# Ends of the layers, low parts in two halves, one chunk taken earlier and query sums in column groups, in a block of two mixer layers and a feed-forward block

## The chip, the cores and the metric

One core of a Trainium2 chip runs the whole program. The metric is the device time in microseconds (us). Five engines matter here: TensorE (PE in the profile, with PEld for its weight loads), VectorE (DVE), ScalarE (ACT), GpSimd (POOL), and SyncE (SP), which only issues the transfers of weights.

## What is computed

The input has 512 rows of 1024 features, all in float32. First come two layers of this form:

```
h    = rms_norm(x) * (1 + scale) + shift
proj = h @ w_in                         # gq gk gv | low rank | gz | dq dk dv dz
o_gla  = rms_norm(gated linear attention(silu(conv(gq, gk, gv)))) * silu(gz)
q, k   = rms_norm(dq) per half head of 64, rms_norm(dk)
attn   = softmax(q1 k1) - lam * softmax(q2 k2)      # 4 heads, causal by chunks
o_diff = rms_norm(attn @ dv) * silu(dz)
x      = x + gate * (concat(o_gla, o_diff) @ w_out)
```

Then follow a gated feed-forward (1024 to 2816 to 1024), a mixer with a spatial gating branch and a short convolution branch, a second feed-forward and a last rms_norm.

## The kernel before

**Products.** Every float32 product of a weight is made as three products of rounded parts (`products`, lines 890 to 897): high weight by high data (L895), high by low (L896), low by high (L897). Where the data are the stationary side the same three stand at L927 to L929. Weights come in chunks of 128 x 2048 (128 x 1408 for the second product of a feed-forward) through two buffers `raw[0]`, `raw[1]`. SP loads a chunk (L463) once the chunk two before it was split. ACT makes its high part `wh` (`take_high`, L543), then POOL its low part `wl` as `raw` minus `wh` in one instruction (`split`, L499), which tells PE and SP through the semaphore `w_ready`.

**Units.** One chunk is one unit of work for PE: two tiles of 128 x 512 in two PSUM banks. `claim` waits until both banks of a unit are emptied, `chunk_ready` until the whole low part is there.

**Layers.** The order inside a layer is a list, `ORDER`, made by `layer_order` (L80). It holds the 56 quarter units ("parts") of the projections, and after part n the small stages that were `put` at n. PE, ACT and DVE all walk the same list in program order; each does its share of a stage. Around the change the list has:

- 29 to 34: sums of squares of the queries. DVE squares them (`q_squares`, L1720), PE sums halves of heads with 16 products of 2 columns from `sq` and 16 from `tmp` (`q_sums`, L1243), ACT takes the root (`q_norm`, L740).
- 35 to 53: 16 attention steps `attn`, each with `score` (L1107), `biases` on DVE (L1627 to L1629, the last of which multiplies two 128 x 2 operands in SBUF into `nbias`), `exps` on ACT, `combine` on DVE (L1639), `turn` (L1116) and `pv` (L1129) on PE.
- 51 to 55: `z_act` (Silu of z on ACT, L768), `gated_r` and `gated_z` (DVE, L1611 and L1619), `diff_ss` (sums for the norm of the attention output, L1604 and L1605), `diff_root` (its root on ACT, L771), and `mix` 0 to 3 (PE transposes at L1082, ACT makes high parts at L658, DVE low parts at L1647).

Behind the list PE waits for the low parts of the first four mixes, claims the banks of both units, and begins the output product with its gla half (`first_out`), with the transposes 4 to 7 of the attention half (`turn_output`) between its pieces. The last quarter of z is emptied by ACT at part 55 (`empty`, L650) straight into Silu; that emptying is what frees the second pair of banks. Behind it ACT takes the next chunk.

**Norms.** `norm(n)` between stages: PE sums squares (L1016, L1020), ACT takes the root (L600) and then the high part of the stage's second chunk, DVE makes a diagonal from two operands in SBUF (L1429), PE spreads it (L1027). For n = 2, 3 and 4 (feed-forward 1, mixer, feed-forward 2; `splits=False`) PE starts the first unit before the norm is known and has the spread behind it.

Of the kernel before, what the change touches and what calls it, by code (L numbers as in the profile page):

```python
# [25 lines left out]
F32 = mybir.dt.float32  # L26
# [5 lines left out]
P = 128  # L32
# [8 lines left out]
HEADS = 4  # L41
# [36 lines left out]
def layer_order():  # L78
# [31 lines left out]
    put(33, "q_squares", (2, 3))  # L110
    put(33, "turn_keys", (0, 1))
    put(34, "q_sums")
    put(34, "turn_keys", (2, 3))
    put(34, "q_norm")
    for s in range(STEPS + 3):
        put(35 + s, "attn", s)
        if s >= 6 and s % 4 == 2:
            put(36 + s, "diff_ss", 3 - (s - 6) // 4)
    for tb in range(TB):
        put(36 + tb, "gated_r", 0, tb)  # L120
    put(51, "z_act", 0)
# [47 lines left out]
def build(nc, ins, out):  # L169
    ctx = ExitStack()  # L170
    with ctx:  # L171
# [32 lines left out]
        inhalf = sb("inhalf", [P, 2])  # L204
        eps = sb("eps", [P, 3])
        sumsq = sb("sumsq", [P, S])
# [116 lines left out]
        w_ready = sem("w_ready")  # L323
        half_used = sem("half_used")
# [44 lines left out]
        q_ss = sem("q_ss")  # L369
        q_scaled = sem("q_scaled")  # L370
# [80 lines left out]
        def _(sp):  # L451
# [31 lines left out]
        def _(pool):  # L483
# [28 lines left out]
        def _(act):  # L512
# [83 lines left out]
            def norm(n, splits=True):  # L596


                act.wait_ge(norm_ss, n + 1)
                nc.scalar.activation(norm_sd[:], ps[:, 6, 0:TB], ACT.Sqrt, bias=eps[:, 0:1],  # L600
                                     scale=1.0 / D).then_inc(norm_root, 1)
                first = (0, CHUNK0["layer1"], CHUNK0["ffn1"], CHUNK0["mixer"], CHUNK0["ffn2"], CHUNKS)[n]
# [13 lines left out]
                take_high(first + 1)  # L616
                if splits:
                    for k in range(KT):
# [10 lines left out]
            for l in range(LAYERS):  # L629
# [58 lines left out]
                for stage, *at_ in ORDER:  # L688
# [45 lines left out]
                    elif stage == "k_norm":  # L734
                        act.wait_ge(k_var, l + 1)
                        nc.scalar.activation(r_qk[:, 0], ss_k[:], ACT.Sqrt, bias=eps[:, 0:1], scale=1.0 / DK
                                             ).then_inc(k_root, 1)
                    elif stage == "q_norm":
                        act.wait_ge(q_ss, l + 1)
                        nc.scalar.activation(r_qk[:, 1].rearrange("p b g -> p (b g)"), ps[:, 5, 0:32], ACT.Sqrt,  # L740
                                             bias=eps[:, 0:1], scale=1.0 / DK).then_inc(q_root, 1)
# [149 lines left out]
        def _(pe):  # L891
# [10 lines left out]

            def chunk_ready(i, chunk, u):
                pe.wait_ge(w_ready, i * 2 + (chunk + u + 1))
# [1076 lines left out]
```

## Time and profile before

| | |
|---|---|
| median of 3 runs | 1829.73 us (1824.44 to 1832.11) |
| the profiled execution, its own time | 1827.28 us |
| its span, first to last instruction | 1825.5 us |
| PE busy | 1760.1 us (96%) |
| DVE, ACT, POOL busy | 939.9, 646.0, 661.9 us |
| mean granted TensorE clock | 0.99 |

Busy PE is not PE at its peak. What is read here is therefore where PE stands idle and what ended each wait, and then, in a timeline of the engines around such a place, what the releaser itself had waited for. In a timeline row the first number is the start, the second the duration, the bracket the idle time ahead and its releaser.

### The profile page before, as it was taken

The numbers are of one execution on the slowest core, as the hardware profiler recorded it, in microseconds if no ns is written. First come the engines' busy times: TensorE is split into PE (matmuls) and PEld (weight loads), VectorE is DVE, ScalarE is ACT, GpSimd is POOL, SyncE is SP. The second block draws the span as 40 slices with busy tenths as digits, with TensorE's granted clock in tenths as the row PEclk, the third lists the DMA queues.
The fourth block names the chain that finished last, engine by engine and source line by source line (L and its number), as shares of the span: only waits on it lengthen the run. The fifth ranks groups of instructions, "written<-read, shape, count | busy, mean of one in ns | idle before, by whom it ended". The sixth has DMA issues, their size and how long they took to land.

```text
span 1825.5 us, 22633 instructions
## 1 busy us (share of the span) xinstructions
PE 1760.1 (96%) x9017; PEld 1447.4 (79%) x9017; DVE 939.9 (51%) x895; ACT 646.0 (35%) x801; POOL 661.9 (36%) x163
## 2 busy tenths in 40 slices
PE   5999999899999999999999999999999999999997
PEld 2677797688888788888888988888888788888885
DVE  4657657777665555554232346672223555554233
ACT  4332563344455433333333332232222433333221
POOL 2232233333222444443444444434444344443442
PEclk9999999899999999999999999999999999999998
DMA  8563112122111222322222332222222222232221
GB/s 335 208 237 108 47 64 74 51 86 74 47 70 47 88 96 92 103 103 70 96 95 87 115 115 92 92 92 92 92 92 92 83 102 92 97 110 71 95 95 62
DMA packets 29660, 180.79 MB, mean 99 GB/s; under 512 B 4342, under 2 KB 4476, under 8 KB 12060
## 3 DMA queue, kind: packets, MB, share of 16 engines
q1 hardware_dynamic: 24480, 161.50, 25.2%
q10 hardware_dynamic: 5116, 18.39, 2.8%
q8 instruction: 46, 0.75, 0.2%
q14 instruction: 18, 0.15, 0.0%
HBM read 177.78 MB, written 2.10 MB: 99 GB/s over the span
## 4 chain that ended last, share of the span: by engine, by line
issue 65%; PE 19%; POOL 15%; POOLq 0%; DVE 0%; ACT 0%; DVEq 0%; ACTq 0%
POOL wl L499 15%; PE ps L897 6%; PE ps L896 6%; PE ps L895 6%; DVE y L1441 0%; POOLq L504 0%; PE ps L1027 0%; POOLq L498 0%; ACT L600 0%; PE ps L1020 0%; DVE sq L1429 0%; DVEq L171 0%; ACT sq L572 0%; POOL glr L487 0%; ACTq L171 0%
## 5 line engine op out<-in xcount | busy, mean ns | idle before, releaser
L499 POOL TENSOR_TENSOR wl<-raw,wh 128x2048 fp32r<-128x2048 f32 (+1 forms) x152 | 659.9, 4342 | 1136.5 <-ACT wh L543 1136.5
L895 PE MATMUL ps<-xh,wh 128*128 128x512 f32 x1280 | 503.8, 394 | 12.9 <-DVE xl L1404 5.6
L896 PE MATMUL ps<-xl,wh 128*128 128x512 f32 x1280 | 499.4, 390 | 0.0
L897 PE MATMUL ps<-xh,wl 128*128 128x512 f32 x1280 | 499.4, 390 | 0.0
L543 ACT ACTIVATE wh<-raw 128x2048 fp32r<-128x2048 f32 x152 | 291.1, 1915 | 495.3 <-PE ps L897 457.7
L895 PEld LDWEIGHTS ps<-xh,wh 128*128 128x128 f32 x1280 | 240.9, 188 | 75.9 <-issue 24.3
L897 PEld LDWEIGHTS ps<-xh,wl 128*128 128x128 f32 x1280 | 240.8, 188 | 51.0
L896 PEld LDWEIGHTS ps<-xl,wh 128*128 128x128 f32 x1280 | 241.1, 188 | 48.9
L1802 DVE TENSOR_TENSOR fl<-tmp,fh 128x512 f32 x44 | 194.9, 4431 | 84.7 <-ACT fh L799 84.7
L927 PE MATMUL ps<-wh,xh 128*128 128x256 f32 x576 | 169.0, 293 | 1.5 <-POOL wl L499 1.5
L928 PE MATMUL ps<-wh,xl 128*128 128x256 f32 x576 | 163.6, 284 | 0.0
L929 PE MATMUL ps<-wl,xh 128*128 128x256 f32 x576 | 163.5, 284 | 0.0
L897 PE MATMUL ps<-fh,wl 128*128 128x512 f32 x352 | 140.4, 399 | 0.0
L896 PE MATMUL ps<-fl,wh 128*128 128x512 f32 x352 | 138.7, 394 | 0.0
L895 PE MATMUL ps<-fh,wh 128*128 128x512 f32 x352 | 138.0, 392 | 0.0
L927 PEld LDWEIGHTS ps<-wh,xh 128*128 128x128 f32 x576 | 110.9, 193 | 20.1 <-issue 19.1
L928 PEld LDWEIGHTS ps<-wh,xl 128*128 128x128 f32 x576 | 111.0, 193 | 0.0
L929 PEld LDWEIGHTS ps<-wl,xh 128*128 128x128 f32 x576 | 110.9, 193 | 0.0
L1418 DVE TENSOR_TENSOR sumsq<-sumsq,sq 128x512 f32<-128x512 f32 x36 | 84.1, 2337 | 41.1 <-ACT sq L572 40.4
L1797 DVE TENSOR_TENSOR tmp<-ps,gate 128x512 f32<-128x512 f32 x44 | 30.5, 692 | 134.0 <-PE ps L897 131.8
L791 ACT ACTIVATE gate<-gate 128x512 f32<-128x512 f32 x44 | 27.9, 633 | 195.8 <-DVE gate L1792 195.8
L1485 DVE TENSOR_TENSOR gate<-ps,r_bc 128x512 f32<-128x512 f32 x16 | 11.1, 691 | 149.6 <-PE ps L897 149.6
(241 smaller groups left out, 2160.5 us busy)
## 6 DMA issues: line engine op xcount, KB each, us to landing
raw<-ffn_in_stream SPq DMA_DIRECT2D x44, 1024.0 KB, 4.8
raw<-mixer_stream SPq DMA_DIRECT2D x40, 1024.0 KB, 4.8
raw<-layer_stream SPq DMA_DIRECT2D x36, 1024.0 KB, 4.9
raw<-ffn_out_stream SPq DMA_DIRECT2D x32, 704.0 KB, 4.1
ada_w<-w_ada SPq DMA_DIRECT2D x8, 1024.0 KB, 18.6
ada_late<-w_ada ACTq DMA_DIRECT2D x16, 512.0 KB, 5.2
ada_late<-w_ada ACTq DMA_DIRECT2D x8, 1024.0 KB, 6.9
x<-x_t SPq DMA_DIRECT2D x1, 2048.0 KB, 7.5
```

The lines of the kernel that those rows point to most:

```text
L499: nc.gpsimd.tensor_tensor(wl[u][:, 0:size], raw[u][:, 0:size], wh[u][:, 0:size].bitcast(F32), ALU.subtract).then_inc(w_ready, 1)
L543: nc.scalar.activation(wh[u][:], raw[u][:], ACT.Copy).then_inc(w_high, 1)
L791: nc.scalar.activation(gate[:, u], gate[:, u], ACT.Silu).then_inc(ff_gate, 1)
L895: nc.tensor.matmul(bank_ap, w0, x0, start=first, stop=False)
L896: nc.tensor.matmul(bank_ap, w0, x1, start=False, stop=False)
L897: return nc.tensor.matmul(bank_ap, w1, x0, start=False, stop=last)
L927: nc.tensor.matmul(dst, xh[:, k, cols], wh[u][:, w], start=(k == 0), stop=False)
L928: nc.tensor.matmul(dst, xl[:, k, cols], wh[u][:, w], start=False, stop=False)
L929: last = nc.tensor.matmul(dst, xh[:, k, cols], wl[u][:, w], start=False, stop=(k == KT - 1))
L1418: ins_ = nc.vector.tensor_tensor(sumsq[:], sumsq[:], sq[:, m % 2], ALU.add)
L1797: nc.vector.tensor_tensor(tmp[:, u], ps[:, 2 * u + 1], gate[:, u], ALU.mult).then_inc(tmp_ready, 1)
L1802: nc.vector.tensor_tensor(fl[:, bass.ds(i * 2 + u, 1)], tmp[:, u:u + 1], fh[:, bass.ds(i * 2 + u, 1)].bitcast(F32), ALU.subtract).then_inc ...
```

## The change

Seven edits.

1. The sums of `diff_ss` 0, the root `diff_root` and both switches of ACT's function table go ahead of mixes 2 and 3, through two one-element activations on a new tile `spare`; the second `z_act` goes from place 54 to 52.
2. PE begins the first gla tile of the output product when the first bank of the last z unit is empty; it claims the rest behind that tile.
3. `split` is two instructions of half the columns; the first signals `half_split`, the second `w_ready`.
4. Units whose tiles use one half each wait for their half only (`half_ready`). Token units, the first unit of a stage and the 1408 column chunks wait for both.
5. For n = 2, 3, 4 `norm` takes the second chunk's high part ahead of the root.
6. The query sums are four products with a 128 x 32 stationary side (`inhalf` widened), one for each head and group of 32 output rows, 512 columns each; ACT copies the bank, PE turns it with four transposes at place 34.
7. The squares of heads 2 and 3 go from place 33 to 32 and the sums from 34 to 33.

```diff
-    put(33, "q_squares", (2, 3))
+    put(32, "q_squares", (2, 3))
+    put(33, "q_sums")
     put(33, "turn_keys", (0, 1))
-    put(34, "q_sums")
+    put(34, "q_turn")
...
-        if s >= 6 and s % 4 == 2:
+        if s >= 6 and s % 4 == 2 and s < STEPS:
             put(36 + s, "diff_ss", 3 - (s - 6) // 4)
...
     put(51, "z_act", 0)
+    put(52, "z_act", 1)
     for tb in range(TB):
         put(52, "gated_z", 0, tb)
-        put(53 + tb // 2, "mix", tb)
-    put(54, "diff_root")
-    put(54, "z_act", 1)
+    put(53, "diff_ss", 0)
+    put(53, "mix", 0)
+    put(53, "mix", 1)
+    put(53, "diff_root")
+    put(54, "mix", 2)
+    put(54, "mix", 3)
...
                 for u in range(2):
+                    sp.wait_ge(half_split, i * 2 + (chunk + u - 1))
                     sp.wait_ge(w_ready, i * 2 + (chunk + u - 1))
...
-                nc.gpsimd.tensor_tensor(wl[u][:, 0:size], raw[u][:, 0:size], wh[u][:, 0:size].bitcast(F32),
-                                        ALU.subtract).then_inc(w_ready, 1)
+                for half in range(2):
+                    cols = slice(half * size // 2, (half + 1) * size // 2)
+                    last = nc.gpsimd.tensor_tensor(wl[u][:, cols], raw[u][:, cols], wh[u][:, cols].bitcast(F32),
+                                                   ALU.subtract)
+                    last.then_inc(half_split if half == 0 else w_ready, 1)
...
+                if not splits:
+                    take_high(first + 1)
                 act.wait_ge(norm_ss, n + 1)
                 nc.scalar.activation(norm_sd[:], ps[:, 6, 0:TB], ACT.Sqrt, bias=eps[:, 0:1],
                                      scale=1.0 / D).then_inc(norm_root, 1)
...
-                take_high(first + 1)
                 if splits:
+                    take_high(first + 1)
...
+                    elif stage == "q_sums":
+                        act.wait_ge(q_rows, l + 1)
+                        nc.scalar.activation(sumsq[:], ps[:, 5], ACT.Copy).then_inc(q_copied, 1)
...
                     elif stage == "diff_root":
+                        nc.scalar.activation(spare[:, 0:1], eps[:, 0:1], ACT.Sqrt)
                         act.wait_ge(o_var, 2 * l + 2)
                         nc.scalar.activation(sd_o[:, 1], ss_o[:, 1], ACT.Sqrt, bias=eps[:, 0:1],
                                              scale=1.0 / P).then_inc(o_root, 1)
+                        nc.scalar.activation(spare[:, 1:2], eps[:, 0:1], ACT.Silu)
...
+            def half_ready(i, chunk, u, half):
+                pe.wait_ge(w_ready if half else half_split, i * 2 + (chunk + u + 1))
+
             def chunk_ready(i, chunk, u):
-                pe.wait_ge(w_ready, i * 2 + (chunk + u + 1))
+                for half in range(2):
+                    half_ready(i, chunk, u, half)
...
             def feature_unit(i, unit, chunk, u, moving):
                 claim(i, unit, u)
-                chunk_ready(i, chunk, u)
                 for t in range(2):
+                    half_ready(i, chunk, u, t)
                     feature_tile(u, t, moving[t])
...
                         for h in range(HEADS):
-                            for tb in range(TB):
-                                last = nc.tensor.matmul(ps[:, 5, tb * 8 + 2 * h:tb * 8 + 2 * h + 2],
-                                                        (sq, tmp)[h // 2][:, h % 2, tb * P:tb * P + P],
-                                                        inhalf[:], start=True, stop=True)
+                            last = nc.tensor.matmul(ps[32 * h:32 * h + 32, 5], inhalf[:], (sq, tmp)[h // 2][:, h % 2],
+                                                    start=True, stop=True)
+                        last.then_inc(q_rows, 1)
+                    elif stage == "q_turn":
+                        pe.wait_ge(q_copied, l + 1)
+                        for tb in range(TB):
+                            last = nc.tensor.transpose(ps[:, 4, tb * P:tb * P + P], sumsq[:, tb * P:tb * P + P], ident[:])
                         last.then_inc(q_ss, 1)
...
                 pe.wait_ge(mix_low, l * 8 + TB)
+                gla = range(HEADS)
+                pe.wait_ge(banks_free[1], emptied(out_unit - 1, 0))
+                half_ready(0, out_unit, 0, 0)
+                first_out(0, 0, gla)
                 for u in range(2):
                     claim(0, out_unit, u)
-                chunk_ready(0, out_unit, 0)
-                gla = range(HEADS)
-                first_out(0, 0, gla)
+                half_ready(0, out_unit, 0, 1)
                 first_out(0, 1, gla)
                 turn_output(4)
                 turn_output(5)
-                chunk_ready(0, out_unit, 1)
+                half_ready(0, out_unit, 1, 0)
                 first_out(1, 0, gla)
```

## Rows read from the trace of the kernel before

**Rows 1.** Waits of TensorE: out, who ended the wait; total us, times, longest

```profile
PE ps L895 <- POOL wl L499: 5.9, 4, 1.8
PE ps L895 <- ACT zg L650: 5.5, 2, 2.7
PE ps L1116 <- DVE prob L1639: 5.2, 6, 1.4
```

**Rows 2.** GpSimd's splits by shape: count, busy us, mean ns, idle before

```profile
L499 POOL TENSOR_TENSOR wl<-raw,wh 128x2048 fp32r<-128x2048 f32 x120 | 556.5, 4637 | 983.6 <-ACT wh L543 983.6
L499 POOL TENSOR_TENSOR wl<-raw,wh 128x1408 fp32r<-128x1408 f32 x32 | 103.4, 3232 | 153.0 <-ACT wh L543 153.0
```

**Rows 3.** Timeline, the first attention step of layer 0

```profile
188.86 4.58 POOL L499 TENSOR_TENSOR wl<-raw,wh 128x2048 fp32r<-128x2048 f32 x1 [14.78 <-ACT wh L543]
189.55 3.91 DVE L1629 TENSOR_TENSOR nbias<-smax,nrq 128x2 f32<-128x2 f32 x1
196.47 0.66 PE L1116 MATMUL ps<-ident,prob 128*128 128x128 f32 x4 [1.39 <-DVE prob L1639]
```

**Rows 4.** Timeline, layer 1: who has the pair of ports next

```profile
379.43 0.75 DVE L1678 SCALAR_TENSOR_TENSOR conv<-u_in,conv_w,conv 128x512 f32<-128x512 f32 x1
379.62 5.00 POOL L499 TENSOR_TENSOR wl<-raw,wh 128x2048 fp32r<-128x2048 f32 x1 [16.16 <-ACT wh L543]
380.22 4.95 DVE L1678 SCALAR_TENSOR_TENSOR conv<-u_in,conv_w,conv 128x512 f32<-128x512 f32 x1
```

**Rows 5.** Timeline, second units of feed-forward 1 and of the mixer

```profile
630.57 4.55 POOL L499 TENSOR_TENSOR wl<-raw,wh 128x2048 fp32r<-128x2048 f32 x1 [14.11 <-ACT wh L543]
635.26 0.47 PE L895 MATMUL ps<-xh,wh 128*128 128x512 f32 x1 [1.76 <-POOL wl L499]
1002.86 0.36 PE L927 MATMUL ps<-wh,xh 128*128 128x256 f32 x1 [1.51 <-POOL wl L499]
```

**Rows 6.** Timeline, third output unit of layer 0

```profile
307.08 0.47 PE L895 MATMUL ps<-mix_h,wh 128*128 128x512 f32 x1 [1.17 <-POOL wl L499]
```

**Rows 7.** Timeline, query sums of both layers, a column group product

```profile
179.40 1.84 PE L1243 MATMUL ps<-inhalf,sq 128*128 128x2 f32 x16
181.11 1.93 PE L1243 MATMUL ps<-inhalf,tmp 128*128 128x2 f32 x16
59.12 1.06 PE L1007 MATMUL ps<-ada_late,c_wide 128*32 128x512 f32 x8 [1.88 <-DMA ada_late<-w_ada]
170.64 3.99 DVE L1604 TENSOR_TENSOR conv<-o_gla 128x512 f32<-128x512 f32 x1
174.99 0.68 PE L1156 MATMUL ps<-states,conv 64*64 64x128 f32 x16
```

**Rows 8.** Busy by window, layer 1: PE, PEld, DVE, ACT, POOL, granted clock

```profile
465.00:470.00 5.00, 5.00 (x36) 5.00 (x37) 0.00 (x0) 0.00 (x0) 0.00 (x0) 0.76 0.00 0
470.00:475.00 5.00, 5.00 (x28) 5.00 (x27) 0.79 (x3) 1.57 (x4) 0.00 (x0) 0.55 0.00 0
570.00:575.00 5.00, 4.73 (x14) 3.82 (x15) 4.97 (x5) 1.81 (x2) 3.11 (x1) 0.66 0.00 0
```

**Rows 9.** Timeline, the end of layer 0

```profile
276.73 1.28 ACT L771 ACT_TABLE_LOAD   x1
279.64 1.06 ACT L768 ACTIVATE zg<-zg 128x1024 f32<-128x1024 f32 x1
278.65 2.87 DVE L1611 TENSOR_TENSOR o_diff<-o_diff,r_o 128x512 f32<-128x512 f32 x4
281.44 0.48 PE L895 MATMUL ps<-mix_h,wh 128*128 128x512 f32 x1 [2.73 <-ACT zg L650]
283.07 4.85 POOL L499 TENSOR_TENSOR wl<-raw,wh 128x2048 fp32r<-128x2048 f32 x1 [12.83 <-ACT wh L543]
287.12 1.03 PE L1082 MATMUL ps<-ident,o_diff 128*128 128x128 f32 x8
```

**Rows 10.** Timeline, layer 0 to layer 1

```profile
337.82 2.72 DVE L1452 TENSOR_SCALAR tmp<-tmp,mod 128x512 f32<-128x512 f32 x1
```

More of the change, by code:

```diff
@@ L203, in build @@
         inchunk = sb("inchunk", [P, 2])
-        inhalf = sb("inhalf", [P, 2])
+        inhalf = sb("inhalf", [P, 32])
         eps = sb("eps", [P, 3])
+        spare = sb("spare", [P, 2])
         sumsq = sb("sumsq", [P, S])
@@ L323, in build @@
         w_ready = sem("w_ready")
+        half_split = sem("half_split")
         half_used = sem("half_used")
@@ L369, in build @@
         q_ss = sem("q_ss")
+        q_rows = sem("q_rows")
+        q_copied = sem("q_copied")
         q_scaled = sem("q_scaled")
@@ L596, in norm @@
             def norm(n, splits=True):
+                first = (0, CHUNK0["layer1"], CHUNK0["ffn1"], CHUNK0["mixer"], CHUNK0["ffn2"], CHUNKS)[n]
+                if not splits:
+                    take_high(first + 1)
                 act.wait_ge(norm_ss, n + 1)
@@ L601, in norm @@
                                      scale=1.0 / D).then_inc(norm_root, 1)
-                first = (0, CHUNK0["layer1"], CHUNK0["ffn1"], CHUNK0["mixer"], CHUNK0["ffn2"], CHUNKS)[n]
                 if n == 0:
@@ L737, in _ @@
                                              ).then_inc(k_root, 1)
+                    elif stage == "q_sums":
+                        act.wait_ge(q_rows, l + 1)
+                        nc.scalar.activation(sumsq[:], ps[:, 5], ACT.Copy).then_inc(q_copied, 1)
                     elif stage == "q_norm":
                         act.wait_ge(q_ss, l + 1)
-                        nc.scalar.activation(r_qk[:, 1].rearrange("p b g -> p (b g)"), ps[:, 5, 0:32], ACT.Sqrt,
-                                             bias=eps[:, 0:1], scale=1.0 / DK).then_inc(q_root, 1)
+                        nc.scalar.activation(r_qk[:, 1].rearrange("p b (h m) -> p b h m", m=2),
+                                             ps[:, 4].rearrange("p (b h r) -> p b h r", b=TB, h=HEADS)[:, :, :, 0:2],
+                                             ACT.Sqrt, bias=eps[:, 0:1], scale=1.0 / DK).then_inc(q_root, 1)
                         act.wait_ge(o_var, 2 * l + 1)
@@ L1062, in part @@
                         pe.wait_ge(banks_free[(unit - 1) % 2], emptied(unit - 1, t))
-                    if p == 0:
-                        pe.wait_ge(w_ready, unit + 1)
                     if stage in ("conv", "q"):
+                        if half == 0:
+                            half_ready(0, unit, 0, t)
                         for k in range(half * KT // 2, (half + 1) * KT // 2):
@@ L1070, in part @@
                     else:
+                        if p == 0:
+                            chunk_ready(0, unit, 0)
                         last = token_block(u, p, 0)
@@ L1098, in out_unit_of @@
                     claim(i, out_unit, u)
-                    chunk_ready(i, out_unit, u)
                     for t in range(2):
+                        half_ready(i, out_unit, u, t)
                         first_out(u, t, range(KT))
@@ L1287, in _ @@
                 turn_output(7)
+                half_ready(0, out_unit, 1, 1)
                 first_out(1, 1, gla)
@@ L1315, in output_tile @@
                     for half in range(2):
+                        pe.wait_ge(half_split, i * 4 + (chunk + 2 * m + half + 1))
                         pe.wait_ge(w_ready, i * 4 + (chunk + 2 * m + half + 1))
@@ L1366, in _ @@
                 claim(i, unit, u)
-                chunk_ready(i, chunk, u)
                 for t in range(2):
                     gate_block(2 * j + t)
+                    half_ready(i, chunk, u, t)
                     feature_tile(u, t, (xh, xl))
```

## The prediction, made before the result was known

> **What bounds the kernel now.** The page comes first: PE is busy for 1760.1 of 1825.5 us, so some 65 us are idle, and everything the other engines do is worth only what it gives back of those or takes off PE's own work. Next the waits of TensorE [rows 1]. Three of them lie where the change works: products that wait for POOL's low part, the product behind the last emptying of z, and the transposes of attention that wait for DVE. Then, for each, the timeline around it, to see what the releaser had waited for. Three things come out.
>
> First, DVE and POOL exclude each other. In [rows 3] a DVE product of 128 x 2 elements, both operands in SBUF, lasts 3.91 us: it begins at 189.55, while POOL's split runs from 188.86 to 193.44, and ends 0.02 behind it. PE then waits 1.39 us for the end of that chain. Who gets its turn next is seen in [rows 4]: POOL asks at 379.62 while a DVE instruction runs to 380.18, the next DVE instruction asks at 380.22, and POOL goes first (it ends at 384.62, the DVE instruction 0.55 later). The one that already waits goes ahead of the next one on the other side.
>
> Second, four places where a unit starts late because a split has just begun or ended [rows 5, 6]. Third, places where PE is busy with little: 32 products of 2 columns in each layer [rows 7], and in layer 1 the granted clock falls there from 2.4 to 1.2 GHz with PE never idle [rows 8].
>
> **Halves, their own price.** The two shapes of split give 4.64 us for 2048 columns and 3.23 for 1408 [rows 2], so 2.2 ns a column and about 0.14 to 0.19 us for an instruction. A half of 2048 takes some 2.4 us, the pair 4.8, and with a DVE instruction let in between 5.4. In all that is some 29 us more on POOL, which is idle for 1136 us ahead of its splits [rows 2]; and in the streaming stages a chunk has the time of a unit to be ready (48 products, at 24 in 5.7 us [rows 9] some 11 us), against 1.6 for the high part (from the emptying's end at 281.44 to the split at 283.07 [rows 9]) and 5.4. Taken as 0 there.
>
> **Attention, both layers.** The DVE product of [rows 3] is let in behind the first half, at about 191.3 instead of 193.44, 2.2 us sooner. PE's wait is 1.39 us, so it goes completely. None of the other five waits of this kind is longer; the six make 5.2 us [rows 1], and each has a split running when its chain begins. Late next is PE itself, busy with parts of v. **Minus 5.2.** From the Trainium skill, SBUF — State Buffer, section Who interferes with whom: a VectorE instruction with two inputs in SBUF and a GpSimd instruction that reads SBUF exclude each other for a whole instruction, and issue order decides who blocks. The trace agrees on the first (3.91 us for 2 columns); what it makes of two halves queued one behind the other is a rival below.
>
> **Second chunk ahead of the root.** Feed-forward 1: PE waits 1.76 us at 635.26 for a split that began at 630.57 [rows 5]. ACT has nothing to do ahead of the sums, so high part and split move 4 to 5 us forward. The waits are 1.76, 1.51 [rows 5] and once more 1.76 in feed-forward 2 (the three and the two of [rows 6] are the waits for `wl` of [rows 1], 5.9 and 1.5 in all). That time ahead of the sums is longer than the high part, so the root isn't later; the diagonal that DVE makes of two operands in SBUF may wait for POOL, but PE comes to its spread 3 us after it. The transfer of that chunk was released by a split long done. **Minus 5.0**; bounds 5.0 and, if the root were pushed back by a whole high part and nothing covered it, 1.6 less for each of the three.
>
> **Output units.** In each layer the third output unit waits 1.17 us for its split [rows 6]; its first tile needs only the first half, 2.2 us sooner, and the second tile comes 5.6 us later. **Minus 2.3.** DVE's sums there are let in earlier, which nothing waits for.
>
> **Query sums.** Removed: 32 products, from 179.40 to 182.9, 3.5 us [rows 7]. Added: four products in four column groups, for which the modulation in the same shape is the nearest row, 8 records in 1.06 us [rows 7], and four transposes, half of the eight in 1.03 us [rows 9]: together 1.6. ACT's copy lies between parts and is covered. The sums are now one place earlier, directly behind the read-out that ends at 175.67 [rows 7], and DVE must have squared the last heads. DVE's instruction ahead of that stood behind a split until 174.63 [rows 7], so the split ended near 174.1 and began 4.6 before; with halves it is let in at 171.9 and the split ends near 174.85, then two squares, 176.0: PE waits 0.35. Gain 3.5 - 1.6 - 0.35 = 1.6, twice: **minus 3.2**. Bounds: nothing if the squares come 1.5 us later, 4 if the wait is none.
>
> **The clock.** In layer 1 the granted clock is 0.76 over 5 us and 0.55 over the next 5 [rows 8]; the stretch at 1.2 GHz begins in the sums of 2 columns, and 0.24 x 5 + 0.45 x 5 = 3.4 us are lost. With dense products in their place I expect no fall: **minus 3.4**, bounds 0 and 3.4, since in layer 0 the same sums brought none. From the Trainium skill, TensorE: Matmul & The Clock Gate, section What's actually happening: the gate goes by how busy the array has been; the trace agrees in so far as the fall came without idle time.
>
> **End of a layer.** This looks like the largest item and is nearly nothing. PE idles 2.73 us before 281.44 [rows 9], because ACT has two table loads, a root and a Silu of 1.06 ahead of the emptying. With the switches moved ahead PE starts at 278.7; the low parts of mixes 2 and 3 come later than before (two loads of 1.28 and the earlier Silu lie ahead of their high parts), near 278.4 by my count, just in time. But see what follows. PE's 24 gla products take 5.7 us (281.44 to 287.12), so it wants transposes 4 and 5 at 284.4. DVE's eight gating instructions can't be sooner than before, since they stand behind those same low parts: four from 278.65 to 281.5, then the `gated_z`. POOL is sooner: the emptying took 0.74 us from 280.70, POOL began 1.63 after it, so now it asks at about 281.1 to 281.3. It had been 283.07, when three of the four `gated_z` were through. Now the first `gated_z` (281.55) meets the first half (to 283.9, ends 284.5), the second one meets the second half (to 286.9, ends 287.4), and transpose 5 wants just that one. The next products start near 287.8 instead of 287.97. **Minus 0.2 a layer, 0.3 in all.** If the first `gated_z` asked 0.3 us sooner than POOL, the second would meet only the first half, end at 285.1, and the gain would be 2.3 a layer. Bounds: minus 2.4 and plus 0.4.
>
> **Layer 0 to 1.** A DVE instruction of 0.5 us lasts 2.72 behind a split [rows 10]; with halves it is sooner and the next one is caught instead. Taken as 0, bounds minus 0.5 and plus 0.3.
>
> **The sum.** 5.2 + 5.0 + 2.3 + 3.2 + 3.4 + 0.3 = 19.4 us. Against the profiled execution: 1827.28 - 19.4 = 1807.9. The median of the runs lies 2.45 above that execution, and the runs spread over 7.7 us, so I carry the same distance: **1810**.
>
> **Rivals.**
>
> *The first `gated_z` wins* at the ends of layers: 4.2 us more off, 1806. For it, the distance is 0.3 us in a count over a dozen steps; against, ACT's new small activations can only make it later. Chance 0.20.
>
> *No hand-over between the halves*: POOL's second half, already in its queue, goes first. By the skill's rule that issue order decides this would come if it counts as issued; [rows 4] speak against it. Then each of the six attention waits becomes 0.2 longer (6.4 us of my sum gone) and the query squares are late by another 0.9 in each layer (1.8 gone): 1818.5. Chance 0.13.
>
> *The clock falls elsewhere*: the places with idle time keep theirs (0.66 over 5 us at the end of layer 1 [rows 8]) and the query sums fall too, as PE waits there now; 3 to 6 us less, 1813 to 1816. Chance 0.09.
>
> *Slower, a half that costs like a whole.* My 1.7 us for a half of 1408 columns comes from a straight line through two sizes. All that the rows bound is that it costs no more than the 3.23 of the whole. In the second products of the feed-forwards a chunk is 33 products, 7.8 us at 5.7 for 24; the high part takes 1.6, a DVE instruction in between 0.6, so from 5.6 us for the pair the splits set the pace. At 6.5 the 32 chunks lose 0.9 each, 29 us in all: 1810 + 29 = 1839. Against it: a fixed part so large would show in the shorter shape. Chance 0.03.
>
> My forecast has the other 0.55.
>
> **How the numbers follow.** The range takes in the won race with a little of the clock (1801) and the missing hand-over with its uncertainty (1821). Within 0.5% (9.1 us) is about what a measurement of this kernel can tell from no change: faster is below 1820.6. The forecast, the won race and the clock case lie there, and two thirds of the missing hand-over: 0.55 + 0.20 + 0.08 + 0.05 = 0.88. Slower 0.03, the rest 0.09.
>
> **What would show it.** After the change: `nbias` never over 2.4 us, and no wait of the transposes L1116; no wait for `wl` at second units and third output units; four products of 512 columns and no fall of the clock in layer 1's sums; at each layer's end no idle time ahead of the gla products but some 2.5 us between the transposes 4 and 5, ended by `gated_z`. I am wrong if `gated_z` comes through at once, if `nbias` still lasts over 3 us, or if POOL's half is far from 2.4.

## The result, and the profile after the change

Before, four runs in the same comparison: median 1830.92 us (1824.44 to 1833.87). After, four runs: median **1798.49 us** (1797.60 to 1799.57), ratio 0.9825, 95% interval 0.9808 to 0.9842. The profiled execution of after took 1799.57 us (span 1797.8), the one of before 1827.28: 27.7 us between these two, 32.4 between the medians. The forecast was 1810 and its range ended at 1801: the time is 11.5 us below the forecast and 2.5 below the range.

Engines of the changed kernel (busy us, share of the span, instructions); then its splits by shape; then TensorE's waits (total us, times, longest):

```profile
PE 1748.9 (97%) x8977; PEld 1438.5 (80%) x8977; DVE 759.2 (42%) x895; ACT 649.3 (36%) x807; POOL 736.7 (41%) x315
```

```profile
L511 POOL TENSOR_TENSOR wl<-raw,wh 128x1024 fp32r<-128x1024 f32 x240 | 619.2, 2602 | 893.7 <-ACT wh L556 893.7
L511 POOL TENSOR_TENSOR wl<-raw,wh 128x704 fp32r<-128x704 f32 x64 | 115.5, 1825 | 140.9 <-ACT wh L556 140.9
```

```profile
PE ps L1019 <- DMA ada_w<-w_ada: 14.2, 3, 11.6
PE ps L1052 <- DVE sq L1463: 9.7, 3, 4.2
PE ps L916 <- DVE xl L1438: 5.8, 5, 4.6
```

All three waits of [rows 1] are gone from the list. What is left above 0.5 us stands at the head of the kernel, at the start of layer 1 and at the end, but for one wait of 1.1 us inside layer 1 that the kernel before has too. Two halves take some 5.2 us where one split took 4.64 [rows 2], and no product waits for them.

I aligned the two executions by TensorE's own marks (first score of each attention step, first transpose of each output, first sum of each norm) and read the time between the starts of the same two instructions, here called "between starts". It moved by: attention -3.5 and -3.7 us in the two layers, ends of layers -2.9 and -4.3 (of the latter 1.7 was clock, [rows 8]), query sums -1.8 and -5.0 (of the latter 3.4 clock), third output units -1.6 each, second chunks -2.0, -1.9 and -2.0, layer 0 to 1 -0.8, and at the head +3.4, where this execution had a stretch at 1.2 GHz and the one of before had none (granted clock from 30 to 50 us 0.74 and 1.00). As rounded these add up to the 27.7.

The attention step of [rows 3], in layer 0 (timeline; start us, duration us):

```profile
190.50 4.73 POOL L511 TENSOR_TENSOR wl<-raw,wh 128x1024 fp32r<-128x1024 f32 x2 [12.38 <-ACT wh L556]
191.19 1.72 DVE L1663 TENSOR_TENSOR nbias<-smax,nrq 128x2 f32<-128x2 f32 x1
```

`nbias` is let in behind the first half, 1.72 us instead of 3.91. The hand-over between halves that the prediction took from [rows 4] shows in the whole kernel: `nbias` lasts at most 1.76 us in its 32 instructions (4.38 before), and the longest DVE instruction of all 3.13 (5.56 before).

The end of layer 0: PE first, then three of DVE's four `gated_z`, then POOL's two halves:

```profile
276.73 0.28 PE L954 MATMUL ps<-wl,xh 128*128 128x256 f32 x1
276.85 0.40 PE L916 MATMUL ps<-mix_h,wh 128*128 128x512 f32 x1
...
282.45 1.22 PE L1109 MATMUL ps<-ident,o_diff 128*128 128x128 f32 x8
...
279.48 0.69 DVE L1653 TENSOR_TENSOR o_diff<-zg,o_diff 128x512 f32<-128x512 f32 x1
280.08 2.88 DVE L1653 TENSOR_TENSOR o_diff<-zg,o_diff 128x512 f32<-128x512 f32 x1
282.89 2.87 DVE L1653 TENSOR_TENSOR o_diff<-zg,o_diff 128x512 f32<-128x512 f32 x1
...
279.52 2.89 POOL L511 TENSOR_TENSOR wl<-raw,wh 128x1024 fp32r<-128x1024 f32 x1 [10.98 <-ACT wh L556]
282.37 2.84 POOL L511 TENSOR_TENSOR wl<-raw,wh 128x1024 fp32r<-128x1024 f32 x1
```

The gla products follow the last one of z at once (276.73, 276.85), where 2.73 us were idle [rows 9]. DVE asks at 279.48 and is through at 280.17; POOL's half is recorded from 279.52 and lasts 2.89, 0.5 more than a half of 2.39 that waits for nobody (it is shown with the first experiment). So **the first `gated_z` won, by 0.04 us**. The second one waits for the first half only and ends at 282.96, and transposes 4 and 5 run as one row of eight. In layer 1 the times are 554.50 and 554.55.

### The profile page after: what moved, and what is told of

Its sections match the earlier page's. It is cut to its first block, busy times and chain, and to the rows that moved or that the text cites. A ratio compares the mean times of both kernels' runs of the same rounds, so it can differ in the third digit from the quotient of the medians.

```text
span 1797.8 us, 22905 instructions
## 1 busy us (share of the span) xinstructions
PE 1748.9 (97%) x8977; PEld 1438.5 (80%) x8977; DVE 759.2 (42%) x895; ACT 649.3 (36%) x807; POOL 736.7 (41%) x315
## 4 chain that ended last, share of the span: by engine, by line
PE 93%; DVE 3%; DMA 2%; ACT 1%; issue 1%; SPq 0%; DVEq 0%; ACTq 0%
PE ps L916 25%; PE ps L917 24%; PE ps L918 24%; PE ps L952 4%; PE ps L954 3%; PE ps L953 3%; DMA ada_w<-w_ada 1%; PE ps L1134 1%; PE ps L1156 1%; PE ps L1032 1%; DVE xl L1438 1%; PE ps L1167 0%; PE ps L1143 0%; PE ps L1109 0%; PE ps L1392 0%
## 5 line engine op out<-in xcount | busy, mean ns | idle before, releaser
L511 POOL TENSOR_TENSOR wl<-raw,wh 128x1024 fp32r<-128x1024 f32 (+1 forms) x304 | 734.7, 2438 | 1034.6 <-ACT wh L556 1034.6
L1836 DVE TENSOR_TENSOR fl<-tmp,fh 128x512 f32 x44 | 100.4, 2282 | 84.7 <-ACT fh L820 84.7
L917 PEld LDWEIGHTS ps<-fl,wh 128*128 128x128 f32 x352 | 66.1, 188 | 16.2
L916 PEld LDWEIGHTS ps<-fh,wh 128*128 128x128 f32 x352 | 66.1, 188 | 15.9
```

Of the source, the lines that this page charges most:

```text
L511: last = nc.gpsimd.tensor_tensor(wl[u][:, cols], raw[u][:, cols], wh[u][:, cols].bitcast(F32), ALU.subtract)
L916: nc.tensor.matmul(bank_ap, w0, x0, start=first, stop=False)
L917: nc.tensor.matmul(bank_ap, w0, x1, start=False, stop=False)
L1836: nc.vector.tensor_tensor(fl[:, bass.ds(i * 2 + u, 1)], tmp[:, u:u + 1], fh[:, bass.ds(i * 2 + u, 1)].bitcast(F32), ALU.subtract).then_inc ...
```

## The experiments

Each kernel ran at least four times beside the kernel before, whose medians were 1829.1 to 1831.9. Where two kernels come from different comparisons, I rest nothing on differences of medians below 2 us unless the traces show them too. The head of the kernel differs by up to 3.5 us from one profiled execution to another; a difference between starts leaves it out.

### The race at the layer's end

One instruction ahead of DVE's reciprocal `r_o[:, 1]`, of one column in the first kernel, of 512 in the second:

```
                             dve.wait_ge(o_root, 2 * l + 2)
+                            link(nc.vector.memset(spare[:, 0:1], 0.0))
```

```
                             dve.wait_ge(o_root, 2 * l + 2)
+                            link(nc.vector.memset(conv[:, 2], 0.0))
```

> The kernel after the change, with one DVE instruction of one column added ahead of the reciprocal of the second units (about 0.1 us for it and its wait), in each layer. Nothing is left out. Theory R (the race): at the ends of layers the first gated_z was asked for at 279.48 us and POOL's first half at 279.52, so that DVE won the two ports by 0.04 us; 0.1 us more turns it round. Then POOL's first half runs ahead of the first gated_z, the second half ahead of the second one, the two transposes of the output that lie between the gla products wait for it, and PE idles some 2.6 us more in each layer: 1798.5 + 5.2 = 1803.7, and 1 to 2 more if the granted clock falls over the idle time. Rival S (no race; the gain at layer ends comes from the earlier start of the gla products alone): the four gated_z have time in hand, at most 0.2 more in all, 1798.7.

> As the one before, with a DVE instruction of 512 columns (some 0.45 us) in place of that of one column. Nothing is left out. It is the same question at five times the delay. Theory R: once the race is lost the price is that of the halves and not of the delay, so the same as with 0.1 us, within 0.5 us: 1803.7 (up to 1805.5 with the clock). Rival S (only the delay itself is handed on, 0.5 us a layer): 1799.5, and five times the loss of the run before.

Measured: 1803.27 us (1802.20 to 1806.25), ratio 0.9858 (0.9838 to 0.9878), and 1806.06 (1804.52 to 1809.07), 0.9879 (0.9857 to 0.9901). The first, 0.1 us later, at the end of layer 0:

```profile
279.77 2.39 POOL L511 TENSOR_TENSOR wl<-raw,wh 128x1024 fp32r<-128x1024 f32 x1 [10.99 <-ACT wh L556]
279.87 2.83 DVE L1653 TENSOR_TENSOR o_diff<-zg,o_diff 128x512 f32<-128x512 f32 x1
282.12 2.79 POOL L511 TENSOR_TENSOR wl<-raw,wh 128x1024 fp32r<-128x1024 f32 x1
282.63 2.83 DVE L1653 TENSOR_TENSOR o_diff<-zg,o_diff 128x512 f32<-128x512 f32 x1
...
282.76 0.66 PE L1109 MATMUL ps<-ident,o_diff 128*128 128x128 f32 x4
285.51 0.66 PE L1109 MATMUL ps<-ident,o_diff 128*128 128x128 f32 x4 [2.10 <-DVE o_diff L1653]
```

This is the picture that the prediction had drawn: each half ahead of one `gated_z`, and PE idle between transposes 4 and 5, 2.10 us. A delay of 0.1 us costs 4.8 us in the medians; rival S had 0.2. Between starts it costs 2.3 us in layer 1 and 3.8 in layer 0, where the clock fell behind the idle time too. Five times the delay has the same 2.1 us of idle time, and between starts its layer ends cost 0.5 us more than the first kernel's in both layers together. Its median lies 2.8 us above the first kernel's, outside what theory R allowed (1805.5 at most), but its profiled execution (1805.39) 0.9 us below the first one's (1806.25); for the medians I give no reason.

### The order and the claims, singly and together

Order: the `put` lines from `z_act` to `mix` as before, the last `diff_ss` back at its step, no spare Sqrt and Silu. Claims:

```
-                pe.wait_ge(banks_free[1], emptied(out_unit - 1, 0))
-                half_ready(0, out_unit, 0, 0)
-                first_out(0, 0, gla)
                 for u in range(2):
                     claim(0, out_unit, u)
+                half_ready(0, out_unit, 0, 0)
+                first_out(0, 0, gla)
```

> The kernel after the change, with the order at the ends of layers as it was (the switch of the table, root and Silu of the second units behind the mixes, the last sums of squares where they were, no spare Sqrt and Silu); the singly claimed banks stay. Nothing is left out. Theory: ACT empties z's last halves late again, PE idles some 2.7 us ahead of the gla products in each layer, POOL's split moves back behind three of the four gated_z, so that nothing is lost to it: 1798.5 + 5.4 = 1803.9, to 1805.6 if the granted clock falls in layer 1 as in the kernel before. Rival (my count of the prediction, where the order was worth 0.3 us): 1799.

> The kernel after the change, with the two claims of banks at the output units together again, ahead of the first gla product, so that its tile waits for both last halves of z; the new order stays. Nothing is left out. Theory T (the two parts of the layer's end do the same thing twice: one takes ACT's chain off the wait, the other puts 12 products of 2.85 us on top of it; either alone is nearly enough): z's last half is emptied 0.8 to 0.9 us behind its last product, so 0.9 us a layer, 1798.5 + 1.8 = 1800.3. Rival A (each part has its own gain, and with the order worth 2.0 as measured, the claims hold the other 5 of the 7.1): 1803.6.

> The kernel after the change, with the order at the layer's end and the claims both as before the change. Nothing is left out. Theory T (substitutes): the 2.7 us of idle time come back whole in each layer, and with idle time of that length the granted clock falls over the products behind it in some executions, 1.5 us each: 1798.5 + 5.4 = 1803.9 without and 1806.9 with both falls, more than the sum of the two single undoings (2.0 + 1.8). Rival A (the parts add): 1798.5 + 2.0 + what the claims alone turn out to be worth, 1802.3 to 1805.6, and no more than that sum.

Measured, as medians above 1798.5: the old order alone +2.0 (1800.53, 1799.71 to 1801.55), the old claims alone +2.4 (1800.87, 1799.55 to 1801.85), both +8.9 (1807.39, 1805.64 to 1808.46; ratio 0.9873, 0.9855 to 0.9892). Between starts it is 0.6 us a layer for the order, 0.9 for the claims and 4.3 for both. My first expectation (+5.4 for the order) was wrong; the ones written after it held, but for the size of the last (8.9 where I had 5.4 to 8.4). Below are the start of the gla products with the old claims, the same with both old, and the granted clock with both old. A row of a window has its limits and length, the busy time of PE, PEld, DVE, ACT and POOL, and then the clock:

```profile
276.03 0.48 PE L916 MATMUL ps<-mix_h,wh 128*128 128x512 f32 x1 [0.89 <-ACT zg L665]
```

```profile
278.45 0.76 PE L910 MATMUL ps<-mix_h,wh 128*128 128x512 f32 x1 [2.74 <-ACT zg L661]
```

```profile
279.00:282.00 3.00, 3.00 (x9) 2.36 (x8) 3.00 (x4) 0.99 (x1) 1.93 (x1) 0.52 0.01 3
558.00:562.00 4.00, 4.00 (x12) 3.13 (x11) 4.00 (x4) 1.16 (x1) 2.76 (x2) 0.57 0.01 4
```

With the claims taken singly, 12 products (2.8 us at 2.4 GHz, from 276.85 to 279.64) need only z's first half and cover ACT's chain, whatever its order; with the new order there is hardly a chain to cover. Either part removes nearly the whole wait: the old claims leave 0.9 us a layer, the old order 0.5, and that for POOL's low part, which comes later. Only with both undone do the 2.74 us come back, and behind them the clock falls to 1.2 GHz over the next products, in both layers.

### The halves

Alone, on the kernel before (every consumer waits for both), and taken out of the kernel after:

```
                 pool.wait_ge(w_high, i * 2 + (chunk + u + 1))
-                nc.gpsimd.tensor_tensor(wl[u][:, 0:size], raw[u][:, 0:size], ...).then_inc(w_ready, 1)
+                for half in range(2):
+                    cols = slice(half * size // 2, (half + 1) * size // 2)
+                    last = nc.gpsimd.tensor_tensor(wl[u][:, cols], raw[u][:, cols], ...)
+                    last.then_inc(half_split if half == 0 else w_ready, 1)
```

> The kernel before with one part of the change alone: each low part is split in two instructions, and every consumer still waits for both. Nothing is left out. Theory H (hand-over between halves): the waits of the transposes in attention go (7.2 us between starts), and 0.8 us at the boundary of layers 0 and 1; units that wait for a split wait 0.2 us longer at five places (+1.0). Against the kernel before: 7 us less, 0.9962; nbias lasts at most 2.4 us. Rival N (the attention gain came from elsewhere, or the halves have a price of their own in the streaming stages): within 2 us of the kernel before, or slower.

> The kernel after the change, with each low part made by one instruction again, every consumer waiting for the whole. Nothing is left out. Theory I (the halves carry much of what the other parts gain): attention +7.2, third output units +3.2, the query squares 0.9 later in each layer +1.8, boundary +0.8, at the layer's end the first gated_z wins but the second one meets a whole split, +2.4 and perhaps 1.5 of clock a layer, +4.8 to 7.8, less 1.0 for five waits that become 0.2 shorter: 1798.5 + 17 to 20 = 1815.5 to 1818. Rival A (the halves are worth here what they are worth alone on the kernel before, 5.0, and their own third output units, 3.2): 1806.7.

Alone: 1824.32 us (1821.99 to 1829.14), 5.0 below the kernel before, ratio 0.9977 (0.9964 to 0.9991). I had expected 7. `nbias` lasts 1.72 us and no wait of the transposes in attention is left; 3.5 us a layer are gone between starts, and 0.8 at the boundary of the layers. What is given back is more than I had counted: its waits for `wl` are 8.1 and 1.7 us in all where before had 5.9 and 1.5, 2.4 more instead of 1.0. The clock doesn't explain the rest: this execution has it down in two places of layer 0 where the profiled one of before had not, but for less time or not at all at the two places of layer 1 [rows 8]. The last 0.6 us stay open.

Taken out: 1816.80 us (1816.00 to 1817.97), **+18.3**, ratio 0.9927 (0.9910 to 0.9945). Between starts the attention loses 3.4 and 3.5, the third output units 1.5 and 1.4, the query squares 0.85 a layer, the layer ends 2.2 each, the boundary 0.9. My expectation of the total held (17 to 20). At the layer ends it was wrong in the cause: POOL's split is recorded at 283.38 and the first `gated_z` at 283.45, so this kernel loses the race, and PE's two waits for the transposes are 2.1 us each. So the halves alone are worth 5, and beside the other parts 18: those use the halves (a first tile that needs only one, squares that come in time), and with whole splits the race is lost as well.

### The earlier second chunk

```
             def norm(n, splits=True):
-                if not splits:
-                    take_high(first + 1)
                 act.wait_ge(norm_ss, n + 1)
...
+                take_high(first + 1)
                 if splits:
-                    take_high(first + 1)
```

> The kernel after the change, with the second chunk behind the root again at the feed-forwards and the mixer. Nothing is left out. Theory: the three waits for the split come back, 1.8 to 2.0 us each from start to start (5.9), and 0.2 more each for the pair of halves, less 2.4 each where the first tile needs only the first half of its chunk, so that little is left in feed-forwards; the mixer's second unit takes the whole chunk. With the halves in place the part is then worth (1.9 + 0.2 - 2.4 < 0) nothing at the two feed-forwards and 2.1 at the mixer: 1800.6. Rival A (the 5.9 come back whole because the second unit waits for both halves or the clock falls at the waits): 1804.4.

> The kernel after the change with two parts undone at once: the low parts by one instruction each, and the second chunk behind the root at the feed-forwards and the mixer. Nothing is left out. It is the fourth corner beside the kernel after the change, the one with whole splits (1816.8) and the one with the chunk behind the root (1799.9). Theory T (the halves and the earlier chunk end the same waits, so the earlier chunk is worth 1.4 with halves and nearly all of its wait without): three waits of 1.5 to 1.8 us, 1.8 to 2.0 from start to start: 1816.8 + 5.7 = 1822.5. Rival A (the parts add; the earlier chunk is worth 1.4 everywhere): 1818.2.

The chunk behind the root again, with halves: 1799.88 us (1799.81 to 1802.75), +1.4. Without halves: 1821.32 us (1820.24 to 1823.53), 4.5 above the kernel with whole splits, nearer to theory T's 5.7 than to rival A's 1.4. Between starts the three waits bring 2.0, 1.7 and 2.0 us without halves, and 1.9 at the mixer alone with them. TensorE's waits for the low part, with halves (one row) and without (two rows):

```profile
PE ps L950 <- POOL wl L511: 1.7, 1, 1.7
```

```profile
PE ps L909 <- POOL wl L507: 5.9, 4, 1.8
PE ps L945 <- POOL wl L507: 1.5, 1, 1.5
```

The 5.9 us hold the third output units of the layers too (2.4). At the feed-forwards the second unit's first tile needs only the first half, and that alone ends the wait; the earlier chunk ends it a second time. It earns its place at the mixer, whose token units take both halves at once.

### The query sums

After with the 32 products of 2 columns back, and before with the four column groups alone:

> The kernel after the change, with the sums of the query squares as before: 32 products of 2 columns, at their old place. Nothing is left out. Every theory: 1.6 to 1.8 us a layer for the products, 3.4 in all, 1801.9. Theory C (products of 2 columns let the granted clock fall, with no idle time): in one layer or both a stretch at 1.2 GHz follows the sums, 3 to 5 us more, some executions without it, so the runs spread over more than 4 us and the median lies at 1804 to 1806. Rival D (the falls of the kernel before needed the idle time around them, which is gone): no such stretch, spread under 3 us, 1801.9.

> The kernel before with one part of the change alone: the sums of the query squares by four products in four column groups, ACT's copy and four transposes, one place earlier. Nothing is left out. Theory C (the 2-column products are what lets the granted clock fall there): 3.4 less for the products and 3.4 less for the fall in layer 1, less some wait for squares that are late without halves (0.9 a layer): against 1829.2 for the kernel before 1822 to 1824, ratio 0.997. The falls behind the idle time at the layers' ends stay, so the spread does too. Rival D (the falls only move on): 1826 to 1828.

Measured: 1807.38 us (1804.90 to 1808.17), +8.9, ratio 0.9875 (0.9858 to 0.9893); and 1825.09 us (1822.33 to 1827.62), 4.2 below the kernel before, ratio 0.9972 (0.9959 to 0.9985). The granted clock of the first, from the old sums on in each layer; of the kernel after around its new sums (453 to 461); and of the second kernel, there and at the end of layer 1:

```profile
184.00:190.00 6.00, 6.00 (x34) 5.11 (x33) 0.90 (x4) 2.65 (x5) 0.00 (x0) 0.72 0.00 0
462.00:470.00 8.00, 8.00 (x41) 7.10 (x41) 0.95 (x4) 2.96 (x5) 0.00 (x0) 0.65 0.01 2
```

```profile
453.00:461.00 8.00, 7.79 (x78) 6.58 (x77) 3.33 (x5) 3.62 (x7) 0.14 (x1) 1.00 0.42 133
```

```profile
463.00:471.00 8.00, 6.93 (x70) 5.72 (x69) 4.63 (x7) 2.84 (x5) 0.07 (x1) 1.00 0.35 133
570.00:574.00 4.00, 4.00 (x12) 3.12 (x11) 4.00 (x4) 1.02 (x1) 2.90 (x1) 0.57 0.02 4
```

With the old sums the clock falls in both layers, though PE is busy all the time (6.00 of 6.00) and the idle time of before around them is gone. The two windows lose 0.28 x 6 + 0.35 x 8 = 4.5 us; in layer 1 the fall begins inside the sums, 1.2 us ahead of the window, which adds some 0.6. With the 3.4 for the products that is 8.5 of the 8.9 measured. The fall doesn't need idle time around it, so rival D of the first falls. Theory C had the direction, not the sizes: it wanted a range over 4 us and a median of 1804 to 1806, and they came out at 3.3 and 1807.4. This run puts the sums back to their old place too, so products of 2 columns and one place later are not told apart.

Alone on the kernel before, the column groups cure the fall behind themselves and not the one behind the idle time at 570. The median of 1825.1 lies between theory C (1822 to 1824) and rival D (1826 to 1828), but the clock of 1.00 over the sums speaks for C. The sums themselves bring only 1.0 us in layer 0 between starts, because without halves PE waits 1.1 us a layer for the squares.

### Two further steps

A Sqrt of one column into a spare tile ahead of each norm's last squares loads the root's table while ACT is idle; and the second chunk ahead of the root at the start of layer 1 too (`if n:` in place of `if not splits:`).

> The kernel after the change, with one instruction more ahead of each norm's last squares: a Sqrt of one column on ACT into a spare tile, so that the table of the root is loaded while ACT has nothing to do. Nothing is left out. In the kernel after the change the root behind the sums is preceded by a table load of 1.28 us each time, and PE then idles 2.74 us ahead of the spread at the start of layer 1 and at the end of the kernel. Theory: both get 1.28 us shorter, the first norm's lies beside the modulation's loads and brings nothing: 1798.5 - 2.6 = 1795.9. Rival (at layer 1 the products wait for the first low part, which is behind POOL's split, and the split's start moves along with the root, so only the end gains): 1797.2.

> The kernel after the change, with the second chunk ahead of the root also at the start of layer 1. Nothing is left out. Theory (why this is another case than the feed-forwards): ACT is free from 324.99 us and the root's table load starts at 326.17, so the high part of 1.90 us pushes the root back by 0.8; the first half of the split then runs from 327.2 and DVE's diagonal behind the root waits for it, 0.6 more; against that the second half is over before the first low part, which gets back 1.3. Net between nothing and 0.3 more: 1798.5 to 1798.9. Rival (a gain as at the feed-forwards, where the waits were 1.5 to 1.8 us): 1797.0.

> The kernel after the change, with the table of each norm's root loaded ahead, and the second chunk ahead of the root at the start of layer 1 too. Nothing is left out. Singly they brought 2.1 and 1.0 us. Rival A (they add): 1795.4. Theory T (at layer 1 they stand in each other's way: with the high part of 1.90 us first, the root comes at 326.9 instead of 326.2, its diagonal meets POOL's first half all the same and is through at 330.2, as without the load; the earlier load then gains only at the end of the kernel): 1797.5 - 1.1 = 1796.4, the same as with the load alone.

Measured: 1796.36 us (1795.90 to 1797.80; ratio 0.9821, 0.9799 to 0.9844), 1797.53 (1797.21 to 1800.16; 0.9830, 0.9807 to 0.9853), and both 1796.63 (1795.61 to 1797.73; 0.9809, 0.9792 to 0.9825). The table load is worth 1.1 us at each of two places between starts. What the chunk brings at the boundary can't be told from nothing by these runs. Together they gain no more than the load alone. The root in the kernel with the load ahead; load, root and diagonal in the kernel after; POOL's first half and the diagonal in the one with both:

```profile
325.77 0.26 ACT L618 ACTIVATE norm_sd<-ps,eps 128x4 f32<-128x4 f32 x1 [1.42 <-PE ps L1050]
```

```profile
326.17 1.28 ACT L616 ACT_TABLE_LOAD   x1 [1.19 <-PE ps L1045]
327.47 0.26 ACT L616 ACTIVATE norm_sd<-ps,eps 128x4 f32<-128x4 f32 x1
328.09 0.69 DVE L1463 TENSOR_TENSOR sq<-ident,norm_r 128x512 f32<-128x512 f32 x1
```

```profile
326.89 2.34 POOL L511 TENSOR_TENSOR wl<-raw,wh 128x1024 fp32r<-128x1024 f32 x1 [7.18 <-ACT wh L556]
327.32 2.46 DVE L1467 TENSOR_TENSOR sq<-ident,norm_r 128x512 f32<-128x512 f32 x1
```

No load is left ahead of the root. With both, the diagonal stands behind POOL's first half, 2.46 us instead of 0.69, as theory T said.

## Why the prediction was wrong, and where it was right

**The end of a layer (0.3 said, 7.1 measured between starts).** This is the step that failed: the prediction let DVE's gating start no sooner than before, "since they stand behind those same low parts", and so put the first `gated_z` at 281.55, behind POOL's request at 281.1 to 281.3. At this place the kernel after is 1.69 us ahead of the one before (z's last product starts at 276.73 and 278.42), so on the clock of [rows 9] POOL asked at 279.52 + 1.69 = 281.21, as counted, and the first `gated_z` at 279.48 + 1.69 = 281.17, 0.38 sooner than said. The two reciprocals ahead of the gating, before and after, show why:

```profile
278.36 0.25 DVE L1765 RECIPROCAL r_o<-sd_o 128x16 f32<-128x16 f32 x1 [0.79 <-ACT sd_o L771]
```

```profile
276.30 0.24 DVE L1799 RECIPROCAL r_o<-sd_o 128x16 f32<-128x16 f32 x1
```

Before, DVE was through with the low parts at 277.57 and stood 0.79 us idle for ACT's root. The change itself moved that root ahead of the mixes, and the reciprocal now follows the low parts at once; these came at 278.07 on the clock of [rows 9], not at 278.4.

Everything turned on the order of the two requests. The mechanism (the one that asks first goes, then they alternate) was right: 0.1 us more on DVE made the predicted picture, idle time and all, and the 4.8 us that it cost are near the 4.2 that the prediction put between the two outcomes. Its own sign of being wrong, `gated_z` coming through at once, is what happened. The text had named the turning point as 0.3 us and gave it 0.20; with a count over a dozen steps, the two outcomes should have stood nearer to even. That this kernel wins by 0.04 us is luck: nothing in the change aims at it. The rival had 4.5 us for both layer ends (0.3 and 4.2 more); the rest of the 7.1 is 1.7 of clock in layer 1 and some 0.3 a layer of the next point; 0.2 us stay open. One reading of the prediction was off without effect: z's last emptying ran from 280.60 to 281.18, not from 280.70 to 281.44, where PE starts.

**The size of a wait (attention 5.2 said, 7.2 measured; third units 2.3 and 3.2; second chunks 5.0 and 5.9).** All mechanisms were right, all sizes short by 0.2 to 0.45 us a piece. The bracket of a row is idle time from the modelled end of the product before, and that end lies behind the moment at which the next one could have started: the product at 276.73 lasts to 277.01 and the next starts at 276.85. In [rows 3] PE started 1.67 us after the start before it, 1.39 by the bracket, where back to back products take 0.12: the wait is worth 1.55. For a row of 512 columns it is 0.17 (0.40 at a pitch of 0.23), and the first product behind a wait takes 0.08 longer (0.48). Over 11 waits that makes 1.8 to 2.7 of these 3.8 us. Two more places of the attention (212.09 and 500.64), whose idle time of 0.05 us the list of waits leaves out, cost 0.23 us each between starts. The rest stays open.

**Query sums (3.2 said, 3.3 measured without the clock) and their clock (3.4, and 3.4).** Both were right; the wait for the squares was 0.21 us instead of 0.35. What the prediction missed is that these falls come and go from one execution to the next: in layer 0 the profiled one of before had none, the one with the old sums in the kernel after had one.

**Layer 0 to 1 (0 said, 0.8 measured).** The next DVE instruction is caught instead, as said, but for 1.86 us and not 2.72:

```profile
332.87 1.86 DVE L1486 TENSOR_SCALAR tmp<-tmp,mod 128x512 f32<-128x512 f32 x1
```

**The halves' own price (0 said)** was right: no product waits for a low part, and a half of 1408 columns takes 1.70 us alone, as the straight line had it.

**From the profiled execution to the median (+2.45 carried, -1.1 found).** Before, the median of four lay 3.6 us above the profiled execution, and the runs spread over 9.4 us; after, over 2.0. The distance was no constant of the kernel. The time of a run goes with its mean granted clock: among 13 runs of the kernel before 0.990 in the one of 1826.3 us and 0.984 in the one of 1834.8, in all four of the kernel after 0.991. Where the clock fell is known of profiled executions alone. There it fell now at one, now at another place behind idle time or tiny products, and those places inside the layers are gone. The head is a place that is left: of the 16 profiled executions of this document 13 have the stretch at 1.2 GHz there, and the one of before is one of the three without. So 1827.28 was a low value to carry a sum from, and the +3.4 at the head and the distance of 3.5 nearly cancel; that the other runs of before had the head's fall is likely and not shown. This closes the 11.5 us: +6.8 (layer ends), +3.8 (waits), +0.9 (boundary and sums), -3.4 (head), +3.5 (distance), 11.6 in all as rounded.

Of the rivals, "the first `gated_z` wins" is the one that happened, though it was priced at 1806, 7.5 us too high. No hand-over, a clock that falls in the query sums all the same, and a half like a whole did not happen. In the 0.88 the clock case and the missing hand-over stand with 0.13 together; from their own chances, 0.09 and two thirds of 0.13, it would be 0.18.

## What to carry to other kernels

Where two engines exclude each other, write down who asks first at each place and by how much; if it is a few tenths, both outcomes are forecasts of their own. Before saying that an instruction can't come sooner, look at what ended the wait just ahead of it, and whether the change moves that. Measure a part both alone and taken out of the whole: here the claims, the order, the halves and the earlier chunk ended each other's waits or fed each other, and the same part was worth 5 or 18 us, 4.5 or 1.4. Count a wait from start to start. Look for clock falls behind each wait that a change removes; their end shows as a narrower spread too.

## What was not expected of the hardware

Who got the pair of ports, DVE or POOL, was decided at 0.04 and 0.05 us, and came out the same each time: in the profiled executions of the kernels with the new order and halves (the two with a delayed DVE aside) the first `gated_z` stands 0.04 to 0.06 us ahead in both layers, in those with whole splits 0.05 to 0.07 behind. One DVE instruction of 0.06 us, 0.1 with what it adds around it, turned it. From the Trainium skill, SBUF — State Buffer, section Who interferes with whom: issue order decides who blocks. The trace agrees (279.48 ahead of 279.52, and 279.77 ahead of 279.87); what happens with a queue on both sides it leaves open, and here they alternate, one instruction each.

The granted clock fell from 2.4 to 1.2 GHz behind 32 products of 2 columns with PE never idle (0.72 and 0.65 over the windows above), and not behind four products of 512 columns one place earlier (1.00). Behind the same 32 products the profiled execution of before had the fall in layer 1 alone.

A Sqrt into a spare tile keeps its table over the squares that follow: the root behind them had no load of its own (the row at 325.77 above). From the Trainium skill, ScalarE: Activation LUTs, section Table sets: the hidden batching unit: cheap functions such as copy are in every set; the trace agrees for the Copy behind the root and shows the same of Square, which the page doesn't name there.
